# Second layer of a four-layer block: head norms' squares on ScalarE, forget gates among the keys' products, transposes between weight units, memory values a tile a step, output projections in two halves of the contraction

## The chip, the cores and the metric

One core of a Trainium2 chip runs the whole program once. The metric is device microseconds of that one execution, lower is better. TensorE (PE) multiplies and transposes, VectorE (DVE) and ScalarE (ACT) work on rows and read PSUM, GpSimd (POOL) works on SBUF only, and SyncE (SP) issues the weight loads.

## The reference, cut to what matters

Four layers over 256 tokens of width 1024, in fp32. Layers 0 and 1 have a mixer, a memory attention, an output projection and a squared-ReLU MLP. Layers 2 and 3 have two other mixers, an output projection and a gated MLP. The change concerns the mixer of layer 1 and the output projection of all four.

```python
# layer 1 (fox_group): forgetting attention with QK norm
proj = h @ w_in
q, k, v, f_logit, xq = jnp.split(proj, [512, 1024, 1536, 1544], axis=-1)
q = rms_norm(q.reshape(B, S, 8, 64), q_gain)
k = rms_norm(k.reshape(B, S, 8, 64), k_gain)
c = jnp.cumsum(jax.nn.log_sigmoid(f_logit + b_f), axis=1)      # causal, per head
s = q @ k.T / 8 + c[query] - c[key];  o = softmax(s) @ v
# memory_group: 4 heads of 128 into 256 memory tokens
k, v = jnp.split(rms_norm(mem, g_mem) @ w_kv, [512], axis=-1)
q = rms_norm(xq...);  k = rms_norm(k...);  y = softmax(q @ k.T / sqrt(128)) @ v
# every layer
x = x + jnp.concatenate([y_mix, y_mem], axis=-1) @ w_out
```

## The kernel before

**Products.** 256 tokens are two tiles `tt` of 128. An fp32 product is made of three fp32r products: high by high, high by low, low by high. Weights arrive in units of 128x1024 (two contraction tiles `j` of 512 columns). `unit` waits for a unit whose high part `whi` was made by ScalarE (`splits` there) and whose low part `wlo` by VectorE (`splits` there). There are NSPLIT = 4 buffers of each, and a buffer is released when the unit after it is begun (`unit_used`). A unit gives 12 products of 512 columns (2 `j`, 2 `tt`, 3 parts); a block of 512 output columns is four units, 48 products. `linear` and `block_of` go unit by unit over both tiles, `by_token` goes through all units for tile 0 and then for tile 1.

**Order.** Every engine runs a program written out by hand, in order. A wait at the head of an engine holds all that stands behind it. Both `splits` run ahead of PE by positions that the code sets: `full(name)` first makes the splits up to `AHEAD` = 3 units beyond the block it is about to read, and then waits for that block. The other waits on VectorE (`dve.wait_ge`) make no splits first.

**Layer 1, on PE:** block q by tile; both transposes of the normalised memory (`turn_norm(4, tt)`, banks 6 and 7, read out into MX); the forget gates f (24 contraction steps of 8 columns, 48 products); block k; the memory keys mk1; the cumulative sum c; blocks v and xq1; 32 transposes of the heads' rows (fqT, fkT) in four pieces; then `attend`. **The head norms** run on GpSimd: it squares 1024 columns into `hrow` (`headnorm`), VectorE sums them (`hsums`), GpSimd takes the power and scales the rows.

**Attention.** `attend` has ten steps here, six for the forgetting heads (fa) and four for the memory (ma1). Step n on PE: what `between` holds, scores of n+1, transposes of the probabilities of n, values of n-1. ScalarE (`soft`) makes the exponentials and copies the transposes, VectorE the maxima. The memory values mv1 are four whole units in `between` of steps 1 to 4.

**Output projection** (`out_proj`, `out_half`): columns 0 to 511 first, with all eight contraction tiles. Contraction tiles 4 to 7 come from the attention's rows, transposed last (`mo0`, `mo1`, `nr2`, `nr3`) and read out by ScalarE (MX_hi) and then VectorE (MX_lo). Columns 512 to 1023 follow by tile. Then comes the norm before the MLP.

Of the kernel before, what the change touches and what calls it, by code (L numbers as in the profile page):

```python
# [24 lines left out]
P = 128  # L25
# [61 lines left out]
def program(nc, a):  # L87
    ctx = ExitStack()
    with ctx:
# [127 lines left out]
        def memT(i, which):  # L217

            return slot(((9, 11), (7, 3))[i][which], 1024)
# [20 lines left out]
        def _(pe):  # L240
# [138 lines left out]

            def windows_by_unit(kv, flat):  # L380
# [62 lines left out]
            def out_rows(tag, tt, lo):  # L443

                turn(f"{tag}.{tt}", 6 + tt, [xn[:, tt, lo + j * P:lo + (j + 1) * P] for j in range(4)])
# [88 lines left out]
            def mem_ready(i):  # L534
                for tt in range(TT):
                    read_out(f"xqT{i}.{tt}")
                    read_out(f"mkT{i}.{tt}")
                    read_out(f"mv{i}.{tt}")
# [6 lines left out]
            def out_proj(L, w, k, first_half, late, second_half):  # L545


                names = [f"out{L}.0.0", f"out{L}.0.1"]
                first_half()
                linear(names, [0, 1], [a[w][0]], 2, tok(MX), 0, KT)  # L550
                late(0)
                linear(names, [0, 1], [a[w][1]], 2, tok(MX), 2, KT, opened=False)
                late(1)
                for tt in range(TT):
                    read_out(f"{second_half}.{tt}")
                linear(names, [0, 1], [a[w][2], a[w][3]], 2, tok(MX), 4, KT, opened=False)
                block_by_token(f"out{L}.1", w, 1, tok(MX), [2, 3], {(1, 3): lambda: turn_norm(k, 0)})

            def out_half(L, w, half, behind=None):


                linear([f"out{L}.0.{tt}" for tt in range(TT)], (0, 1), [a[w][2 * half + u] for u in range(2)], 2, tok(MX),
                       4 * half, KT, opened=(half == 0), behind=behind)
# [89 lines left out]
            for tt in range(TT):  # L653
# [8 lines left out]
            out_proj(0, "w_o0", 2, lambda: pe.wait_ge(ev("ylo"), 1),  # L662
                     lambda tt: (read_out(f"ma0.o{tt}"), out_rows("mo0", tt, 512)), "mo0")
# [19 lines left out]
            block_of("xq1", "w_b", 3, tok(XT), [0, 1])  # L683
            for n, s, e in (("fq", 4, "qaug"), ("fk", 7, "kaug")):
                pe.wait_ge(ev(e), 1)
                read_out("c")
                rows = slot(s, 1040).rearrange("p (t h d) -> p t h d", t=2, h=8)
                for tt in range(TT):
                    for half in range(2):
                        turn(f"{n}T.{tt}.{half}", 6 + half, [rows[:, tt, 4 * half + h, :] for h in range(4)])  # L690
# [8 lines left out]
            def mem_values(u):  # L699

                linear(["mv1.0", "mv1.1"], [2, 3], [a["w_kv1"][4 + u]], 2, tok(MX), 2 * u, KT, opened=(u == 0))
# [5 lines left out]
                "ma1": mem_spec(1)}, {**{1 + u: (lambda u=u: mem_values(u)) for u in (0, 2, 3)},  # L707
                                      2: lambda: (mem_values(1), mem_queries(1)), 5: lambda: (mem_keys(1), mem_ready(1)),
                                      9: lambda: [(read_out(f"fa.o{tt}"), out_rows("fo", tt, 0)) for tt in range(TT)]})
            out_proj(1, "w_o1", 5, lambda: [read_out(f"fo.{tt}") for tt in range(TT)],  # L710
                     lambda tt: (read_out(f"ma1.o{tt}"), out_rows("mo1", tt, 512)), "mo1")
# [3 lines left out]
            for L in (2, 3):  # L715
# [182 lines left out]
                def last_rows():  # L898
                    pe.wait_ge(ev("nrow"), i + 1)
                    out_rows(f"nr{L}", 1, 512)  # L900

                hgrn_read()
                out_half(L, f"w_o{L}", 0, {0: lambda: (read_out(f"co{L}.0"), out_rows(f"nr{L}", 0, 512)), 1: last_rows})
                for tt in range(TT):
                    read_out(f"nr{L}.{tt}")
                out_half(L, f"w_o{L}", 1)
                block_by_token(f"out{L}.1", f"w_o{L}", 1, tok(MX), [2, 3], {(1, 3): lambda: turn_norm(k + 1, 0)})
# [22 lines left out]
        def _(act):  # L930
# [233 lines left out]
            for tt in range(TT):  # L1164
                copy_out(f"q.{tt}", slot(0, 1024)[:, tt * BLK:(tt + 1) * BLK])
# [5 lines left out]
            for n, s in (("k", 1), ("mk1", 5), ("v", 2), ("xq1", 3)):  # L1171
                for tt in range(TT):
                    copy_out(f"{n}.{tt}", slot(s, 1024)[:, tt * BLK:(tt + 1) * BLK])
            for n, s in (("fq", 8), ("fk", 10)):
                dst = scr[:, s * SLOT:s * SLOT + 2048].rearrange("p (h t) -> p h t", h=8)
                for tt in range(TT):
                    for half in range(2):
                        copy_out(f"{n}T.{tt}.{half}", dst[0:65, 4 * half:4 * half + 4, tt * P:(tt + 1) * P],
                                 lambda ps: ps[0:65, :].rearrange("p (h t) -> p h t", h=4))
# [310 lines left out]
        def _(dve):  # L1490
# [316 lines left out]
            for tt in range(TT):  # L1807
                norm_rows(4, tt, slot(8 + tt, 1024))
# [444 lines left out]
```

## Time and profile before

| | us |
|---|---|
| median of 3 runs | 1411.62 |
| lowest, highest | 1409.45, 1412.41 |
| the profiled execution | 1406.15 |
| its span, first to last instruction | 1404.4 |
| PE busy in it | 1340.6 |
| DVE, ACT, POOL busy | 874.6, 712.6, 151.1 |

The profiled execution is one run and lies 5.5 us below the median of the three timed ones; 1.75 us of it lie outside the span. PE busy time counts a matmul from start to modelled end, so PE is hardly ever idle in the views and yet its pace depends on its granted clock.

### The profile page before, as it was taken

The numbers are of one execution on the slowest core, as the hardware profiler recorded it, in microseconds if no ns is written. First come the engines' busy times: TensorE is split into PE (matmuls) and PEld (weight loads), VectorE is DVE, ScalarE is ACT, GpSimd is POOL, SyncE is SP. The second block draws the span as 40 slices with busy tenths as digits, with TensorE's granted clock in tenths as the row PEclk, the third lists the DMA queues.
The fourth block names the chain that finished last, engine by engine and source line by source line (L and its number), as shares of the span: only waits on it lengthen the run. The fifth ranks groups of instructions, "written<-read, shape, count | busy, mean of one in ns | idle before, by whom it ended". The sixth has DMA issues, their size and how long they took to land.

```text
span 1404.4 us, 18621 instructions
## 1 busy us (share of the span) xinstructions
PE 1340.6 (95%) x7251; PEld 1136.1 (81%) x7251; DVE 874.6 (62%) x1146; ACT 712.6 (51%) x1167; POOL 151.1 (11%) x176
## 2 busy tenths in 40 slices
PE   6879999999998999999999999999999999999998
PEld 5657888887876788887988878888889887788887
DVE  4885656656443665656776556666677656666665
ACT  6465544545454554445653445555565444555553
POOL 2211100003340400002011011000021010100000
PEclk9989999998999999999999999999999999999999
DMA  9433655554521556554741136555556321466651
GB/s 374 140 119 97 232 196 192 168 181 157 172 92 60 195 169 206 191 184 152 242 135 60 61 105 208 187 190 190 166 170 208 112 61 60 140 194 194 193 194 46
DMA packets 62328, 224.44 MB, mean 160 GB/s; under 512 B 7192, under 2 KB 7328, under 8 KB 62240
## 3 DMA queue, kind: packets, MB, share of 16 engines
q1 hardware_dynamic: 59616, 214.23, 45.6%
q0 software_dynamic: 1904, 6.82, 1.5%
q10 hardware_dynamic: 720, 2.19, 0.4%
q8 instruction: 58, 0.95, 0.3%
q14 instruction: 30, 0.25, 0.1%
HBM read 222.16 MB, written 1.05 MB: 159 GB/s over the span
## 4 chain that ended last, share of the span: by engine, by line
PE 80%; DVE 11%; ACT 4%; issue 2%; POOL 2%; DMA 0%; POOLq 0%; DVEq 0%; ACTq 0%
PE ps L277 15%; PE ps L323 15%; PE ps L281 15%; PE ps L282 14%; PE ps L327 8%; PE ps L423 3%; DVE wlo L1502 2%; PE ps L330 2%; PE ps L481 2%; PE ps L458 2%; PE ps L753 2%; PE ps L329 1%; ACT scr L994 1%; DVE xn L1541 1%; POOL small L1327 1%
## 5 line engine op out<-in xcount | busy, mean ns | idle before, releaser
L1502 DVE TENSOR_TENSOR wlo<-raw,whi 128x1024 fp32r<-128x1024 f32 (+1 forms) x402 | 480.2, 1216 | 254.3 <-ACT whi L940 252.4
L940 ACT ACTIVATE whi<-raw 128x1024 fp32r<-128x1024 f32 (+1 forms) x409 | 424.3, 1048 | 314.6 <-PE ps L323 178.6
L323 PE MATMUL ps<-XT,whi 128*128 128x512 f32 x896 | 318.7, 399 | 0.0
L327 PE MATMUL ps<-XT,wlo 128*128 128x256 f32 x896 | 251.6, 281 | 0.0
L323 PEld LDWEIGHTS ps<-XT,whi 128*128 128x128 f32 x896 | 168.4, 188 | 41.1
L277 PE MATMUL ps<-whi,HT_hi 128*128 128x512 f32 (+1 forms) x496 | 187.8, 379 | 2.8 <-DVE wlo L1502 2.2
L282 PE MATMUL ps<-whi,HT_lo 128*128 128x512 f32 (+1 forms) x496 | 186.3, 376 | 0.0
L281 PE MATMUL ps<-wlo,HT_hi 128*128 128x512 f32 (+1 forms) x496 | 186.2, 375 | 0.0
L327 PEld LDWEIGHTS ps<-XT,wlo 128*128 128x128 f32 x896 | 169.2, 189 | 1.2
L277 PE MATMUL ps<-whi,XT 128*128 128x512 f32 (+2 forms) x352 | 141.2, 401 | 10.2 <-DVE wlo L1502 7.9
L281 PE MATMUL ps<-wlo,XT 128*128 128x512 f32 (+2 forms) x352 | 136.6, 388 | 0.0
L282 PE MATMUL ps<-whi,XT 128*128 128x512 f32 (+2 forms) x352 | 136.1, 387 | 0.0
L277 PEld LDWEIGHTS ps<-whi,HT_hi 128*128 128x128 f32 x496 | 93.2, 188 | 20.6 <-DVE wlo L1502 3.7
L282 PEld LDWEIGHTS ps<-whi,HT_lo 128*128 128x128 f32 x496 | 93.2, 188 | 17.4
L281 PEld LDWEIGHTS ps<-wlo,HT_hi 128*128 128x128 f32 x496 | 93.2, 188 | 16.9
L994 ACT ACTIVATE scr<-ps,small 128x256 f32<-128x256 f32 (+1 forms) x96 | 47.4, 502 | 98.8 <-DVE small L1591 87.3
L277 PEld LDWEIGHTS ps<-whi,XT 128*128 128x128 f32 x352 | 69.5, 198 | 28.4 <-DVE wlo L1502 11.1
L277 PE MATMUL ps<-whi,MX_hi 128*128 128x512 f32 x192 | 78.6, 410 | 14.0 <-issue 7.0
L1337 POOL TENSOR_SCALAR small<-small 128x1 f32<-128x1 f32 x20 | 11.0, 550 | 648.0 <-ACT xn L977 647.9
L282 PEld LDWEIGHTS ps<-whi,XT 128*128 128x128 f32 x352 | 69.4, 197 | 13.3
L281 PEld LDWEIGHTS ps<-wlo,XT 128*128 128x128 f32 x352 | 69.6, 198 | 10.3
L281 PE MATMUL ps<-wlo,MX_hi 128*128 128x512 f32 x192 | 76.1, 396 | 0.0
(252 smaller groups left out, 1871.3 us busy)
## 6 DMA issues: line engine op xcount, KB each, us to landing
raw<-in_w_m SPq DMA_DIRECT2D x152, 512.0 KB, 4.2
raw<-in_w_n SPq DMA_DIRECT2D x108, 512.0 KB, 4.2
raw<-in_w_c SPq DMA_DIRECT2D x48, 512.0 KB, 4.1
raw<-in_w_o SPq DMA_DIRECT2D x32, 512.0 KB, 3.6
raw<-in_w_kv SPq DMA_DIRECT2D x16, 512.0 KB, 4.6
raw<-in_w_b SPq DMA_DIRECT2D x16, 512.0 KB, 3.6
raw<-in_w_w SPq DMA_DIRECT2D x16, 512.0 KB, 5.0
raw<-in_w_a SPq DMA_DIRECT2D x12, 512.0 KB, 7.5
```

Source lines behind the costliest of these rows:

```text
L277: m = pe.matmul(out, xh, wh, start=first, stop=False)
L281: pe.matmul(out, xh, wl, start=False, stop=False)
L282: return pe.matmul(out, xl, wh, start=False, stop=last)
L323: m = pe.matmul(outs[f][:, :], hi[:, j, at], both, start=(k == 0), stop=False)
L327: pe.matmul(outs[f][:, 0:T], lo[:, j, at], XT[0][:, k, :], start=False, stop=False)
L330: m = pe.matmul(outs[f][:, :], hi[:, j, at], both, start=False, stop=True)
L423: m = pe.transpose(out[0:f, at:at + p], t, ident[0:p, 0:p])
L458: m = pe.matmul(out[:, j * klen:(j + 1) * klen], qT(h0 + j)[0:kd, tt * P:(tt + 1) * P], kT(h0 + j)[0:kd, 0:klen], start=(j == 0 or not cau ...
L481: m = pe.matmul(out[:, h * hd:(h + 1) * hd], turned(tag, n)[:, (j * kt + t) * P:(j * kt + t + 1) * P], V(h, t), start=(t == 0), stop=(t == ...
L940: act.activation(whi[:, g % NSPLIT, 0:w], raw[:, g % NRAW, 0:w], ACT.Copy).then_inc(split_hi, 1)
L994: m = act.activation(probs(tag, n)[:, j * klen:(j + 1) * klen], src, ACT.Exp, bias=sm(f"nmax{which}", 16)[:, c:c + 1], accum_out=sm(f"rsum ...
L1502: dve.tensor_tensor(wlo[:, g % NSPLIT, 0:w], raw[:, g % NRAW, 0:w], whi[:, g % NSPLIT, 0:w].bitcast(F32), ALU.subtract).then_inc(split_lo, 1)
```

## The change

Five edits in the programs of four engines.

1. **Head norms.** ScalarE squares each block out of PSUM, just before it copies it (`rows_in`). VectorE sums (`fox_sums`), GpSimd only takes the powers, and VectorE scales the rows (`scaled`). The gains become a per-partition column (`fgcol`, `mgcol`), made on VectorE after the logarithm and used as the scale of the copies of fkT and mkT.
2. **Gates among the keys** (`keys_and_gates`): the first keys' unit stands directly behind q; the 48 gate products stand in four groups of 12 among the second unit's; `turn_norm(4, 0)` and `turn_norm(4, 1)` follow the second and third unit.
3. **Turns between units**: the four pieces of fqT and fkT stand behind the four units of xq1.
4. **Memory values a tile a step**: eight pieces of six products (`by_tile`), the first behind the scores of step 0, the others woven into steps 0 to 5; the keys' transposes move from step 5 to 3, the forgetting rows' transposes from 9 to 8, and the first two units of the output projection go into steps 9 and 10.
5. **Output projections** of all layers: contraction tiles 0 to 3 for all 1024 columns (`out_first`, banks 0, 1 and 4, 5), then tiles 4 to 7 for all columns by tile (`out_second`).

```diff
+            def keys_and_gates():
+                names, tokens = ["k.0", "k.1"], tok(XT)
+                outs = [fill(n, b) for n, b in zip(names, (2, 3))]
...
+                for u in range(4):
+                    if u == 1:
+                        gf, fh, fl, _ = unit(a["w_f"][0], KT)
+                        forget = [fill(f"f.{tt}", 4 + tt) for tt in range(TT)]
+                    g, hi, lo, w = unit(a["w_b"][4 + u], 2)
...
+                    if u == 1:
+                        turn_norm(4, 0)
+                    if u == 2:
+                        turn_norm(4, 1)
-            def out_proj(L, w, k, first_half, late, second_half):
-                names = [f"out{L}.0.0", f"out{L}.0.1"]
-                first_half()
-                linear(names, [0, 1], [a[w][0]], 2, tok(MX), 0, KT)
-                late(0)
-                linear(names, [0, 1], [a[w][1]], 2, tok(MX), 2, KT, opened=False)
-                late(1)
-                for tt in range(TT):
-                    read_out(f"{second_half}.{tt}")
-                linear(names, [0, 1], [a[w][2], a[w][3]], 2, tok(MX), 4, KT, opened=False)
-                block_by_token(f"out{L}.1", w, 1, tok(MX), [2, 3], {(1, 3): lambda: turn_norm(k, 0)})
+            def out_first(L, w):
+                for nb, banks in enumerate(((0, 1), (4, 5))):
+                    names = [f"out{L}.{nb}.{tt}" for tt in range(TT)]
+                    for u in range(2):
+                        linear(names, banks, [a[w][4 * nb + u]], 2, tok(MX), 2 * u, KT, opened=(u == 0))
+                        yield
+            def out_second(L, w, k, rows):
+                for tt in range(TT):
+                    read_out(f"{rows}.{tt}")
+                late = lambda t, tt: tok(MX)(t + 4, tt)
+                by_token([([f"out{L}.{nb}.{tt}" for tt in range(TT)], None, [a[w][4 * nb + 2 + u] for u in range(2)], 2, late,
+                           False, True) for nb in range(2)], {(1, 3): lambda: turn_norm(k, 0)})
...
             block_by_token("q", "w_b", 0, tok(XT), [0, 1], after_norm(3), True)
-            for tt in range(TT):
-                turn_norm(4, tt)
-            linear(["f.0", "f.1"], [4, 5], [a["w_f"][0]], KT, tok(XT))
-            block_of("k", "w_b", 1, tok(XT), [2, 3])
+            keys_and_gates()
...
+            block_of("xq1", "w_b", 3, tok(XT), [0, 1],
+                     {0: lambda: heads_turned("fq", 4, 0), 1: lambda: heads_turned("fq", 4, 1),
+                      2: lambda: heads_turned("fk", 7, 0), 3: lambda: heads_turned("fk", 7, 1)})
...
+            def values_tile(n, s):
+                if (n, s) in ((0, 1), (1, 0), (2, 0), (3, 0), (4, 0), (5, 0), (5, 1)):
+                    next(values_left)
...
-                "ma1": mem_spec(1)}, {**{1 + u: (lambda u=u: mem_values(u)) for u in (0, 2, 3)},
-                                      2: lambda: (mem_values(1), mem_queries(1)), 5: lambda: (mem_keys(1), mem_ready(1)),
+                "ma1": mem_spec(1)}, {2: lambda: mem_queries(1), 3: lambda: mem_keys(1), 5: lambda: mem_ready(1, 2),
+                                      7: lambda: mem_ready(1), (8, 1): fox_rows, (9, 2): fox_out,
+                                      10: lambda: (mem_rows(0), next(out_left))},
+                   weave=values_tile, first=lambda: next(values_left))
...
+            def rows_in(name, sq, dst):
+                for tt in range(TT):
+                    at = slice(tt * BLK, (tt + 1) * BLK)
+                    ps = full(f"{name}.{tt}")
+                    act.activation(sq[:, at], ps[:, :], ACT.Square).then_inc(ev("sqf"), 1)
+                    copy_out(f"{name}.{tt}", dst[:, at])
...
+            def fox_sums(n, dst, sq, hd):
+                dve.wait_ge(ev("sqf"), 2 * n)
+                dve.tensor_reduce(dst, sq.rearrange("p (n d) -> p n d", d=hd), AX.X, ALU.add).then_inc(ev("fsum"), 1)
+            def scaled(dst, src, r, n, hd, event):
+                dve.wait_ge(ev("frstd"), n)
+                dve.tensor_tensor(dst, src.rearrange("p (n d) -> p n d", d=hd), bc(r, 2, hd), ALU.mult).then_inc(ev(event), 1)
+            squares_ = hrow[:, :, :].rearrange("p a b -> p (a b)")
+            fox_sums(1, sm("rq16", 16), squares_, 64)
             for tt in range(TT):
                 norm_lo(4, tt, MX)
+            qa = slot(4, 1040).rearrange("p (n d) -> p n d", d=65)
+            dve.memset(qa[:, :, 64:65], 1.0)
+            scaled(qa[:, :, 0:64], slot(0, 1024), sm("rq16", 16), 1, 64, "qaug")
...
+            splits(fills["k.1"].pos + AHEAD)
+            fox_sums(2, sm("rk16", 16), slot(10, 1024), 64)
```

**VectorE where block q ends and the keys begin.** The rows are VectorE's instructions in program order. The four `xn<-scr` normalise the memory rows, `wlo` 128x64 is the gates' unit, and each `wlo` 128x1024 is the low part of a weight unit that PE needs. Before, they read:

```order
L1541 SCALAR_TENSOR_TENSOR xn<-scr,small,gain 128x512 x4
L1502 TENSOR_TENSOR wlo<-raw,whi 128x64
L1502 TENSOR_TENSOR wlo<-raw,whi 128x1024 x2
L1525 TENSOR_TENSOR MX_lo<-ps,MX_hi 128x4x128 x4
L1502 TENSOR_TENSOR wlo<-raw,whi 128x1024
```

After:

```order
L1615 SCALAR_TENSOR_TENSOR xn<-scr,small,gain 128x512 x4
L1887 TENSOR_REDUCE small<-hrow 128x16
L1576 TENSOR_TENSOR wlo<-raw,whi 128x1024
L1576 TENSOR_TENSOR wlo<-raw,whi 128x64
L1576 TENSOR_TENSOR wlo<-raw,whi 128x1024 x4
L1599 TENSOR_TENSOR MX_lo<-ps,MX_hi 128x4x128 x2
L1576 TENSOR_TENSOR wlo<-raw,whi 128x1024
L1599 TENSOR_TENSOR MX_lo<-ps,MX_hi 128x4x128 x2
```

The first keys' unit is now the first `wlo` 128x1024, and the sum over q's squares stands ahead of it; the seventh unit of this list (counting the gates') is the memory keys' second.

**VectorE behind the logarithm of the gates.** The last rows of the logarithm are those of 128x16; what follows is the low part of the memory keys' third unit. Before:

```order
L1696 TENSOR_SCALAR small<-small 128x16
L1823 TENSOR_SCALAR small<-small 128x16
L1824 TENSOR_TENSOR small<-small 128x16
L1502 TENSOR_TENSOR wlo<-raw,whi 128x1024 x8
L1827 TENSOR_SCALAR scr<-ps 128x16
```

After:

```order
L1914 TENSOR_TENSOR small<-small 128x16
L1917 TENSOR_TENSOR small<-rowg 128x64
L1918 TENSOR_TENSOR small<-small,const 128x64
L1919 TENSOR_REDUCE small<-small 128x1
L1920 MEMSET small 1x1
L1921 TENSOR_TENSOR small<-rowg 128x128
L1922 TENSOR_TENSOR small<-small,const 128x128
L1923 TENSOR_REDUCE small<-small 128x1
L1576 TENSOR_TENSOR wlo<-raw,whi 128x1024
L1887 TENSOR_REDUCE small<-scr 128x16
L1576 TENSOR_TENSOR wlo<-raw,whi 128x1024 x4
```

Seven instructions for the two gain columns and the keys' sum have moved in among the low parts; before, the logarithm stood ahead of the low part of the keys' fourth unit and of the seven after it.

**PE at the first attention step, after.** `scr` rows are scores (128x128) and transposes, the 128x512 by `HT_hi` is the mask, `whi` and `wlo` are the first tile of the memory values.

```order
L490 MATMUL ps<-scr 128x128 x4
L494 MATMUL ps<-HT_hi 128x512
L277 MATMUL ps<-whi,MX_hi 128x512
L281 MATMUL ps<-wlo,MX_hi 128x512
L282 MATMUL ps<-whi,MX_lo 128x512
L277 MATMUL ps<-whi,MX_hi 128x512
L281 MATMUL ps<-wlo,MX_hi 128x512
L282 MATMUL ps<-whi,MX_lo 128x512
L490 MATMUL ps<-scr 128x128 x4
```

Before, the two groups of scores stood next to each other, and the first memory value unit followed the first transposes. On VectorE the maximum of step 0 stands ahead of this unit's `wlo` in both kernels.

## Rows read from the trace of the kernel before

**Rows 1.** The page: TensorE's granted clock in 40 slices of the span, tenths.

```profile
PEclk9989999998999999999999999999999999999999
```

**Rows 2.** Waits of PE, 325 to 470 us: total, times, longest.

```profile
PE ps L423 <- DVE MX_lo L1525: 3.4, 2, 1.7
PE ps L423 <- ACT scr L955: 3.2, 5, 1.2
PE ps L458 <- ACT scr L955: 2.3, 2, 1.2
PE ps L277 <- issue: 1.5, 1, 1.5
PE ps L277 <- DVE wlo L1502: 1.3, 2, 0.9
PE ps L423 <- ACT scr L994: 1.2, 1, 1.2
```

**Rows 3.** Busy time per engine in stretches; third from last the clock.

```profile
340.00:345.00 5.00, 5.00 (x22) 4.81 (x23) 0.79 (x5) 0.35 (x2) 0.00 (x0) 0.50 0.33 111
345.00:350.00 5.00, 5.00 (x14) 3.84 (x13) 3.74 (x16) 0.97 (x2) 0.00 (x0) 0.50 0.00 0
430.00:435.00 5.00, 4.99 (x35) 4.25 (x34) 2.50 (x6) 3.65 (x13) 0.00 (x0) 1.00 0.02 3
```

**Rows 4.** Timeline of PE, q's end to v's begin: start, duration, operation.

```profile
332.58 0.40 PE L282 MATMUL ps<-whi,XT 128*128 128x512 f32 x1
...
336.53 0.25 PE L277 MATMUL ps<-whi,XT 128*128 128x8 f32 x1
...
339.66 0.28 PE L281 MATMUL ps<-wlo,XT 128*128 128x8 f32 x1
...
357.73 0.39 PE L277 MATMUL ps<-whi,MX_hi 128*128 128x512 f32 x1
...
369.19 0.48 PE L277 MATMUL ps<-whi,XT 128*128 128x512 f32 x1
```

**Rows 5.** Timeline of PE: eight transposes between products.

```profile
317.23 1.04 PE L423 MATMUL ps<-const,xn 128*128 128x128 f32 x8
318.02 0.48 PE L277 MATMUL ps<-whi,HT_hi 128*128 128x512 f32 x1
```

**Rows 6.** Timeline of DVE: memory rows' low part, logarithm's ends, a sum.

```profile
336.91 1.29 DVE L1525 TENSOR_TENSOR MX_lo<-ps,MX_hi 128x512 fp32r<-128x512 f32 x2 [0.91 <-ACT MX_hi L961]
...
344.02 0.17 DVE L1816 TENSOR_TENSOR small<-ps,rowg 128x8 f32<-128x8 f32 x1 [0.47 <-PE ps L282]
...
347.92 0.18 DVE L1824 TENSOR_TENSOR small<-small 128x16 f32<-128x16 f32 x1
...
376.09 1.22 DVE L1572 TENSOR_REDUCE small<-hrow 128x16 f32<-128x1024 f32 x1 [5.41 <-POOL hrow L1358]
```

**Rows 7.** Timeline of ACT: the copy of q's second tile.

```profile
333.01 0.60 ACT L955 ACTIVATE scr<-ps 128x512 f32<-128x512 f32 x1
```

**Rows 8.** Timeline of PE: heads' transposes, scores of steps 0 and 1.

```profile
392.24 1.04 PE L423 MATMUL ps<-const,scr 128*65 128x128 f32 x8
393.56 1.14 PE L423 MATMUL ps<-const,scr 128*65 128x128 f32 x8 [0.29 <-ACT scr L955]
...
398.63 1.13 PE L458 MATMUL ps<-scr 65*128 65x128 f32 x8 [1.20 <-ACT scr L955]
```

**Rows 9.** Timeline of DVE: maximum of step 0 and splits behind it.

```profile
400.03 0.69 DVE L1587 TENSOR_REDUCE small<-ps 128x4 f32<-128x512 f32 x1 [15.67 <-PE ps L462]
400.63 3.49 DVE L1502 TENSOR_TENSOR wlo<-raw,whi 128x1024 fp32r<-128x1024 f32 x3
```

**Rows 10.** Waits of PE in the whole span, for the output projections.

```profile
PE ps L277 <- issue: 7.0, 5, 1.5
```

**Rows 11.** Timeline of PE in layer 0: a long wait for a low part.

```profile
79.58 0.47 PE L277 MATMUL ps<-whi,MX_hi 128*128 128x512 f32 x1 [2.96 <-DVE wlo L1502]
...
80.34 0.62 PE L277 MATMUL ps<-whi,MX_hi 128*128 128x512 f32 x1
```

More of the change, by code:

```diff
@@ L217, in memT @@
         def memT(i, which):
-            return slot(((9, 11), (7, 3))[i][which], 1024)
+            return slot(((9, 11), (7, 4))[i][which], 1024)
         xflat = xn[:, :, :].rearrange("p t d -> p (t d)")
@@ L543, in mem_spec, with out_proj @@
                         lambda h, t: mv[:, t * BLK + h * P:t * BLK + (h + 1) * P], [2, 3])
[L545 to L563 removed]
+            def out_first(L, w):
[5 more added lines that the diff above has]
+            def out_second(L, w, k, rows):
+                for tt in range(TT):
+                    read_out(f"{rows}.{tt}")
+                late = lambda t, tt: tok(MX)(t + 4, tt)
+                by_token([([f"out{L}.{nb}.{tt}" for tt in range(TT)], None, [a[w][4 * nb + 2 + u] for u in range(2)], 2, late,
+                           False, True) for nb in range(2)], {(1, 3): lambda: turn_norm(k, 0)})
+            def out_proj(L, w, k, late, rows):
+                left = out_first(L, w)
+                for tt in range(TT):
+                    next(left)
+                    late(tt)
+                for _ in left:
+                    pass
+                out_second(L, w, k, rows)
             def mlp(L, w_in, w_out, blocks, kts, squared, k, first=(4, 5)):
@@ L1177, in _, with mem_keys_in @@
                     for half in range(2):
-                        copy_out(f"{n}T.{tt}.{half}", dst[0:65, 4 * half:4 * half + 4, tt * P:(tt + 1) * P],
-                                 lambda ps: ps[0:65, :].rearrange("p (h t) -> p h t", h=4))
+                        ps = full(f"{n}T.{tt}.{half}")
+                        kw = {"scale": sm("fgcol", 1)[0:65, :]} if n == "fk" else {}
+                        free(f"{n}T.{tt}.{half}", act.activation(
+                            dst[0:65, 4 * half:4 * half + 4, tt * P:(tt + 1) * P],
+                            ps[0:65, :].rearrange("p (h t) -> p h t", h=4), ACT.Copy, **kw))
+            rows_in("xq1", squares_, slot(3, 1024))
+            def mem_keys_in():
+                for tt in range(TT):
+                    ps = full(f"mkT1.{tt}")
+                    free(f"mkT1.{tt}", act.activation(
+                        memT(1, 1).rearrange("p (h t) -> p h t", h=4)[:, :, tt * P:(tt + 1) * P],
+                        ps[:, :].rearrange("p (h t) -> p h t", h=4), ACT.Copy, scale=sm("mgcol", 1)))
             def mem_rows_in():
```

147 lines of the change are left out of this document (87 added, 60 removed).

## The prediction

> **What bounds the kernel now.** I read the page first. PE is busy in 1340.6 of the span of 1404.4 us (the table), and its clock is granted in full but for a few slices [rows 1]. Its work is not changed: every product of before is there after, in another order. So a gain can come only from PE's waits and from its stretches at half clock, and a loss only from new ones. The second view is the waits of PE in layer 1 [rows 2]: 12.9 us. The third is the clock in stretches of 5 us: 0.50 in 340 to 350 [rows 3], which is the lower of its two levels (1.2 GHz for 2.4). What PE did before: a wait of 1.7 us for MX_lo [rows 2] and then products of 8 columns [rows 4]. At half clock 10 us of work are 5 of it; about 4.9 us are lost there. The waits of the output projections are the "issue" rows [rows 10]: four of them are 1.53 us, one in each layer; PE stands there until the last transposed rows are read out by ScalarE and VectorE.
>
> All sums below are made against the profiled execution (1406.15 us, span 1404.4) and then put on the median of the runs, 1411.62, which lies 5.5 us higher.
>
> **1. From q to the memory keys.** Before, PE begins q's last product at 332.58 and the memory keys at 357.73 [rows 4]; q's end at 332.81 makes 24.9 us. After, the work is: 48 products of 512 columns, 48 of 8 columns, two groups of eight transposes. From mk1's begin at 357.73 to v's at 369.19 are 48 wide products and the small ones of c [rows 4], so 48 take some 10.9 us (0.227 each). From 336.53 to 339.66 are 28 narrow ones [rows 4], 0.112 each, 5.4 us for 48. Eight transposes in the midst of products take 0.79 us and make the next product 0.1 longer [rows 5]: 1.8 for two groups. Together 18.1 us at full clock, with neither the wait of 1.7 nor the half clock.
>
> But there is a new wait in front. The keys' first unit now stands directly behind q, and VectorE makes its low part only after the sum of q's squares, as the order in the section on the change shows, and the sum waits for the square of q's second tile. Before, this unit was not wanted until the gates were done. q's last product ends at 332.98 (332.58 + 0.40) [rows 4], ScalarE is there at 333.01 and a pass over 128x512 of PSUM takes 0.60 [rows 7]: square done at 333.6. The sum takes 1.22 [rows 6], the low part 1.22 (a little over a third of the 3.49 for three) [rows 9], the second begins 0.1 before the first ends: 336.0. PE begins at 336.07, 3.1 us after q's last end. So mk1 begins at 336.07 + 18.1 = 354.2 instead of 357.73: **3.5 us gained**. Bounds: a wait of 2.0 us (the square and sum overlapping more than I see) gives 4.6; for the clock see rival A.
>
> **2. The memory keys and what stands behind.** With X the begin of the keys' fourth unit (right behind the last transposes), PE wants mk1's third unit at X + 2.75 + 2 x 2.75 = X + 8.25. VectorE: the memory rows' low part ended 1.67 us after the transposes before (336.91 + 1.29 against 336.53) [rows 4, 6], so X + 1.67; clearing a column 0.1; scaling q, a pass over 128x1024 like a low part, 1.2: X + 2.95. Then bias and logarithm: from the second bias to the end 344.02 to 348.10, 4.1 us [rows 6], and 0.15 for the first bias: X + 7.2. Seven operations on 64 and 128 columns for the gains: each 0.18 like the ones of 16 columns [rows 6] and up to 0.12 more for the columns, with the 0.03 between them 1.8: X + 9.0. Low part 1.2: X + 10.2. **PE waits 1.9 us** in mk1, where it waited for nothing. Bounds 1.2 (small operations at 0.18) and 2.6 (twice the seven's excess). Gone is the wait of 0.87 in v, since VectorE stood then for GpSimd's squares (5.41 us) [rows 6] and these are gone. Net **1.0 us lost**. The keys' sum and the scaling of k and mk1, 1.2 us each, find 2.75 us per unit of which a low part takes 1.2; four buffers hide them. ScalarE's eight squares, 0.6 each, come beside its copies; a unit costs it one split in 2.75 us and it is busy in half the span (the table); hidden. The cover would be gone only if they stood in front of a split that PE wants next, which is so for none but the one above.
>
> **3. Turns of the heads.** From 392.24 to 398.63, 6.4 us [rows 8]. After: four times 0.9 [rows 5] and the wait of 1.20 for the last copies, which stays [rows 8], and 0.25 of drain: 5.0. **1.4 us gained**. The copies of fk carry a scale column; bound 0.2 us on the last wait.
>
> **4. Attention.** Of the 12.9 us of rows 2, 1.7 are part 1's, 1.3 for `wlo` are v's 0.9 and 0.4 before the MLP, which stays; the heads have 1.20 and three short ones like the 0.29 [rows 8], 0.8 together. 7.9 us are left, six waits of 1.1 to 1.7: for the exponentials of step 0, the memory keys' copies (two), around the forgetting rows' transposes (two), and before the output projection's second half. All lie where no unit's products stand; now tiles or units do, or (the last) 5.5 us of units. New ones: (a) the first memory tile stands behind the scores of step 0, and its low part on VectorE behind the maximum of step 0. That maximum begins at 400.03 and what follows it at 400.63 [rows 9]; 1.22 later is 401.85, while PE is through with the scores and the mask when the maximum begins: **1.9 us**, since low part and maximum must both be waited for. (b) the second piece of xqT needs bank 7, whose copy stands behind a split and two exponentials on ScalarE: about 0.7, bounds 0 and 1.5. (c) the transposes of step 9 stand behind ScalarE's two MX_hi and exponentials, 0.4. Net 7.9 - 3.0 = **4.9 us gained**.
>
> **5. Output projections of layers 0, 2 and 3.** 1.53 us each [rows 10], now behind two units (5.5 us): **4.6 us gained**. The norm behind them has the same way as before, since the last four pieces by tile take as long as those of the second half did; its additions of the first columns come later, 2.7 us before the second ones, enough for the 0.7.
>
> **Sum:** 3.5 - 1.0 + 1.4 + 4.9 + 4.6 = 13.4 us. I keep 1 us back for short waits that come with 20 new switches between operations. 1411.62 - 12.4 = **1399.2 us** (as a profiled run 1393.8).
>
> **The clock.** In the profile a wait of 2.96 us was followed by half clock (the same product 0.47 long at 79.58 and 0.62 at 80.34) [rows 11], while attention steps without filler, full of small operations, held the full one at 430 to 435 [rows 3]. So the gates among wide products should hold it, and the new wait of 3.1 us need not. The Trainium skill, "TensorE: Matmul & The Clock Gate", section "Why this matters for your kernels", warns of idle gaps of PE between bursts, after which its clock falls; the trace has the case above for it. By that rule rival A is the forecast; I leave it second, since a wait may fall so that it is diluted by the dense products on both sides, which it has here.
>
> **Rivals.** *A. The clock falls at the new wait.* For: [rows 11]. Once for 3 to 4 us it costs 1.7; if it holds on through the gates (the narrow products held it down before) [rows 3] 8.1 us of unit two become 16.2, so up to 9. The time is 1401 to 1408. Chance 0.22. *B. The new waits of 3.1, 1.9 and 1.9 do not show,* since VectorE is earlier than I work out; then 6.9 us more: 1392. Against it stands the order of VectorE, which is fixed. Chance 0.07. *C. No change:* the units moved up meet late low parts wherever a wait vanished, as in (a), each for its like; 1411.6. It needs 12 us more in waits of 1 to 2, some seven more places than I find. Chance 0.04. *D. Slower: the clock at half from the new wait to the end of mk1.* Transposes and gates keep it down and the wait in mk1 comes before it has risen. Work of 18.1 + 10.9 us at full clock doubles: 29 us, 15.7 more than the gain, 1428; it decides from 26 us at half clock on. Against: after the gates 14 wide products at half clock brought it back before [rows 3]. Chance 0.03; 0.02 more for other losses. The forecast itself, with its own range of 1394.5 to 1403, has 0.62.
>
> **The numbers.** 0.2% (2.8 us) is about what a measurement of this kernel can tell from no change. Bounds of the forecast: 1.1 in part 1, 0.7 in 2, 1.0 in 3 and 4 each way, and 2 us since the timed runs lie up to 2.2 us off their median. The range 1393.5 to 1406 takes the forecast and most of A, leaving out 0.17. Faster 0.92 (forecast, A, B), same 0.03, slower 0.05.
>
> **What would show it.** Right: PE's first wide product with XT after q waits some 3 us for `wlo` of VectorE, with a sum from `hrow` right before it there; a wait of 1.9 in mk1 behind seven small operations; one of 1.9 behind the mask of step 0; no "issue" wait of 1.5 in any layer; the clock 1.00 during the gates. Wrong: half clock there (A), or several waits for `wlo` in the output projections, which would mean that their units come sooner than the splits can.

## The result, and the profile after

The changed kernel takes 1406.12 us in the median of 20 runs (1390.98 to 1407.63), the kernel before 1409.88 in 20 runs beside them (1404.70 to 1412.41). The ratio is 0.9969, 95% interval 0.9955 to 0.9983: 4.4 us faster by it (3.8 by the two medians), where 12.4 were forecast. The profiled execution took 1405.79, its span is 1403.7, with a mean granted clock of 0.979; before, 1404.4 and 0.985.

The page after, PE's line and the clock in 40 slices, against [rows 1]:

```profile
PE 1345.6 (96%) x7251; PEld 1141.0 (81%) x7251; DVE 877.5 (63%) x1156; ACT 716.4 (51%) x1175; POOL 131.3 (9%) x163
...
PEclk9999999997999999999999999999999998999999
```

The waits of PE from 325 to 470 us in the changed kernel, against [rows 2]:

```profile
PE ps L277 <- DVE wlo L1576: 7.2, 4, 3.2
PE ps L490 <- ACT scr L1254: 1.4, 1, 1.4
PE ps L455 <- ACT scr L1058: 0.5, 1, 0.5
PE ps L455 <- ACT scr L1019: 0.3, 1, 0.3
```

They are 9.4 us instead of 12.9; 0.5 of the difference is a wait of block q for `wlo` that lies just inside this window before (325.87) and just outside it after (323.47). The timeline of PE after: the last unit of layer 0's output projection, then q's end and the gates, then three later waits (against [rows 4, 8]):

```profile
127.09 0.50 PE L277 MATMUL ps<-whi,MX_hi 128*128 128x512 f32 x1 [0.56 <-DVE wlo L1576]
...
330.18 0.39 PE L282 MATMUL ps<-whi,XT 128*128 128x512 f32 x1
333.73 0.76 PE L277 MATMUL ps<-whi,XT 128*128 128x512 f32 x1 [3.17 <-DVE wlo L1576]
...
338.56 0.63 PE L282 MATMUL ps<-whi,XT 128*128 128x512 f32 x1
...
339.80 0.25 PE L277 MATMUL ps<-whi,XT 128*128 128x8 f32 x1
...
340.79 0.40 PE L281 MATMUL ps<-wlo,XT 128*128 128x512 f32 x1
...
343.21 0.63 PE L282 MATMUL ps<-whi,XT 128*128 128x512 f32 x1
...
345.20 0.35 PE L282 MATMUL ps<-whi,XT 128*128 128x8 f32 x1
...
366.56 0.50 PE L277 MATMUL ps<-whi,MX_hi 128*128 128x512 f32 x1 [1.49 <-DVE wlo L1576]
...
399.84 1.13 PE L490 MATMUL ps<-scr 65*128 65x128 f32 x8 [1.43 <-ACT scr L1254]
...
403.37 0.77 PE L277 MATMUL ps<-whi,MX_hi 128*128 128x512 f32 x1 [2.01 <-DVE wlo L1576]
```

The waits stand where they were forecast and have nearly the sizes forecast: 3.17 behind q (3.1), 1.49 in mk1 (1.9), 2.01 in step 0 (1.9). But the same wide product takes 0.63 us behind the wait at 338.56, 0.40 at 340.79, and 0.63 again at 343.21 in the midst of the gates, and a narrow one goes from 0.25 to 0.35. Those are the two levels of the clock. The same stretch in windows, with the clock third from last (against [rows 3]):

```profile
330.00:335.00 5.00, 1.83 (x6) 1.25 (x5) 3.62 (x4) 2.08 (x4) 2.99 (x3) 0.76 0.40 133
335.00:340.00 5.00, 5.00 (x18) 4.04 (x18) 1.22 (x1) 1.35 (x2) 2.65 (x1) 0.55 0.95 338
340.00:345.00 5.00, 5.00 (x32) 4.63 (x31) 1.23 (x1) 0.35 (x1) 0.00 (x0) 0.79 0.43 161
345.00:350.00 5.00, 5.00 (x22) 4.71 (x22) 0.00 (x0) 0.00 (x0) 0.00 (x0) 0.50 0.00 0
350.00:355.00 5.00, 5.00 (x21) 4.25 (x21) 2.77 (x4) 3.20 (x4) 0.00 (x0) 0.69 0.17 46
...
400.00:405.00 5.00, 2.99 (x13) 2.27 (x13) 3.60 (x4) 3.48 (x12) 0.00 (x0) 0.59 0.11 25
```

Between q and the memory keys 17.1 us are at half clock, where 10.2 were before and none was forecast: 6.8 from 332.6, which is inside PE's wait (330.57 to 333.73), and 10.2 from 342.9, among the gates (338.99 to 350.03). Another 6.8 us from 400.9 lie about the two waits at the attention's begin.

Why the waits are there is read from DVE's timeline after, against [rows 6, 9]: the addition to x stands ahead of the projection's last low part, the sum of q's squares ahead of the keys' first, the gains' operations ahead of mk1's third, the maximum of step 0 ahead of the first memory value unit's.

```profile
125.21 0.69 DVE L1627 TENSOR_TENSOR x<-ps,x 128x512 f32<-128x512 f32 x1 [2.84 <-PE ps L282]
125.82 1.22 DVE L1576 TENSOR_TENSOR wlo<-raw,whi 128x1024 fp32r<-128x1024 f32 x1
...
331.23 1.22 DVE L1887 TENSOR_REDUCE small<-hrow 128x16 f32<-128x1024 f32 x1 [1.24 <-ACT hrow L1234]
332.37 2.48 DVE L1576 TENSOR_TENSOR wlo<-raw,whi 128x1024 fp32r<-128x1024 f32 x3
...
363.57 0.22 DVE L1917 TENSOR_TENSOR small<-rowg 128x64 f32<-128x64 f32 x1
...
365.29 1.22 DVE L1576 TENSOR_TENSOR wlo<-raw,whi 128x1024 fp32r<-128x1024 f32 x1
...
401.40 0.69 DVE L1661 TENSOR_REDUCE small<-ps 128x4 f32<-128x512 f32 x1 [14.66 <-PE ps L494]
402.00 3.49 DVE L1576 TENSOR_TENSOR wlo<-raw,whi 128x1024 fp32r<-128x1024 f32 x3
```

In the output projections the four "issue" waits of 1.53 us [rows 10] are gone, and a new one of 0.56 stands in each.

The two profiles by stage. The stages end at the begin of q's last product, of mk1, of the attention's first scores, of the products behind layer 2's first wait of 1.52 us (734.43 before, 732.65 after), and at the end of the span:

| stage ends at | before, us | after, us | difference | forecast | at half clock, before / after |
|---|---|---|---|---|---|
| q's last product | 332.58 | 330.18 | -2.4 | -1.5 | 10.2 / 6.8 |
| mk1 | 25.15 | 29.29 | **+4.1** | -3.5 | 10.2 / 17.1 |
| attention | 40.90 | 40.37 | -0.5 | -0.4 | 0 / 0 |
| layer 2's wait | 335.80 | 332.81 | -3.0 | -4.9 | 0 / 6.8 |
| end | 669.97 | 671.05 | **+1.1** | -3.1 | 20.5 / 27.3 |

At half clock are 41.0 us before and 58.0 after, which costs 8.5 us more than before. The forecast of the profile was -13.4 before the reserve: 4.9 of it was half clock regained, and 8.5 was waits. The profile shows -0.7. With the 8.5 lost to the clock put aside that is -9.2, close to the 8.5 forecast for the waits. So what lies between forecast and profile, 12.7 us, is the clock: 8.5 lost in place of 4.9 regained.

The sum can be put to the runs, too, since each has its own span and mean clock. A run loses about (1 - clock) x span to half clock; the rest is the span at full clock. In the median that rest is 1382 us for the kernel before (the 17 runs beside the first experiments) and 1374.3 after (20 runs): 7.6 gained. The loss to the clock is 25.4 before and 29.5 after. So 7.6 - 4.1 = 3.5 us are left, about what was measured. Each clock is given to 0.001, so the two parts of a single run are known to about 0.7 us.

### The profile page after: what moved, and what is told of

It is laid out like the page before. It is cut to its first block, busy times and chain, and to the rows that moved or that the text cites. A ratio compares the mean times of both kernels' runs of the same rounds, so it can differ in the third digit from the quotient of the medians.

```text
span 1403.7 us, 18627 instructions
## 1 busy us (share of the span) xinstructions
PE 1345.6 (96%) x7251; PEld 1141.0 (81%) x7251; DVE 877.5 (63%) x1156; ACT 716.4 (51%) x1175; POOL 131.3 (9%) x163
## 4 chain that ended last, share of the span: by engine, by line
PE 79%; DVE 12%; ACT 4%; issue 2%; POOL 2%; DMA 0%; POOLq 0%; DVEq 0%; ACTq 0%
PE ps L323 15%; PE ps L277 15%; PE ps L282 14%; PE ps L281 14%; PE ps L327 8%; DVE wlo L1576 3%; PE ps L455 3%; PE ps L330 2%; PE ps L513 2%; PE ps L490 2%; PE ps L818 2%; PE ps L329 1%; ACT scr L1058 1%; DVE xn L1615 1%; DVE x L1627 1%
## 5 line engine op out<-in xcount | busy, mean ns | idle before, releaser
L277 PE MATMUL ps<-whi,MX_hi 128*128 128x512 f32 x192 | 80.4, 419 | 12.4 <-DVE wlo L1576 10.4
L282 PEld LDWEIGHTS ps<-whi,XT 128*128 128x128 f32 x352 | 69.6, 198 | 13.4
L281 PEld LDWEIGHTS ps<-wlo,XT 128*128 128x128 f32 x352 | 69.8, 198 | 10.2
L282 PE MATMUL ps<-whi,MX_lo 128*128 128x512 f32 x192 | 77.4, 403 | 0.0
```

Of the source, the lines that this page charges most:

```text
L277: m = pe.matmul(out, xh, wh, start=first, stop=False)
L281: pe.matmul(out, xh, wl, start=False, stop=False)
L282: return pe.matmul(out, xl, wh, start=False, stop=last)
```

## The experiments

**Theory 1:** TensorE's clock falls at its idle time behind q, and products there would hold it. **Theory 2:** the gates' narrow products bring it down by themselves. All kernels but projection_halves_alone, which is made from the kernel before, are made from the changed kernel. The kernel before ran beside them: 1411.02 us in the median of 17 runs for the experiments 1 to 4, 1410.81 (14 runs) for 5 to 8, 1409.90 (18 runs) for the next three and 1411.02 (9 runs) for the last. The last two columns are on the mean granted clock of each kernel's runs.

| kernel | median us | ratio, 95% | median clock | runs at 0.987 or above |
|---|---|---|---|---|
| the changed kernel | 1406.12 | 0.9969 (0.9955-0.9983) | 0.979 | 2 of 20 |
| projection_halves_alone | 1407.56 | 0.9986 (0.9972-1.0) | 0.981 | 0 of 11 |
| q_sum_behind_splits | 1395.69 | 0.9898 (0.9877-0.992) | 0.9865 | 2 of 4 |
| gates_over_two_units | 1402.08 | 0.9936 (0.9917-0.9955) | 0.984 | 0 of 6 |
| splits_and_two_units | 1398.92 | 0.9922 (0.9904-0.994) | 0.985 | 0 of 4 |
| wait_filled | 1398.08 | 0.9895 (0.9857-0.9932) | 0.9855 | 3 of 6 |
| gates_as_before | 1405.12 | 0.9954 (0.9938-0.9969) | 0.979 | 0 of 9 |
| early_value_half | 1391.69 | 0.9858 (0.9834-0.9882) | 0.988 | 3 of 6 |
| four_orders_mended | 1387.72 | 0.9829 (0.9802-0.9857) | 0.9865 | 3 of 6 |
| four_waits_filled_b | 1398.37 | 0.993 (0.9906-0.9955) | 0.989 | 5 of 7 |
| late_waits_filled_b | 1408.27 | 0.9989 (0.9963-1.0014) | 0.980 | 1 of 12 |
| mended_and_filled_b | 1386.80 | 0.9834 (0.9821-0.9846) | 0.991 | 3 of 4 |
| mended_one_fill | 1386.01 | 0.9824 (0.9804-0.9844) | 0.986 | 1 of 5 |

**1. The sum of q's squares behind the low parts.** On VectorE:

```diff
             squares_ = hrow[:, :, :].rearrange("p a b -> p (a b)")
+            splits(fills["q.1"].pos + AHEAD)
             fox_sums(1, sm("rq16", 16), squares_, 64)
```

> The changed kernel, with VectorE making the low parts of the keys' first unit, the gates' unit and the keys' second ahead of the sum of q's squares. Everything else stays. The wait of 3.17 us behind q should go in every theory. Theory 1 (the wait alone brings the clock down, the gates among wide products can hold it): half clock goes from the whole stretch 332 to 353, about 3.2 + 3.4 + 5.1 = 11.7 us less than the changed kernel, ratio to the kernel before about 0.989. Theory 2 (twelve narrow products between three wide ones bring it down by themselves): only the wait and the first fall go, 6.6 us less, ratio about 0.992, and half clock still stands in the gates.

1395.69 us, 10.4 less than the changed kernel for one line. By its time alone it is nearer to theory 1 (11.7 less) than to theory 2 (6.6 less). The wait behind q is 0.70 instead of 3.17. The windows of this run:

```profile
330.00:335.00 5.00, 4.30 (x20) 3.27 (x19) 4.48 (x6) 3.68 (x6) 1.10 (x2) 1.00 0.16 64
335.00:340.00 5.00, 5.00 (x36) 4.57 (x35) 2.83 (x3) 1.06 (x1) 4.04 (x2) 1.00 0.95 369
340.00:345.00 5.00, 5.00 (x29) 4.68 (x27) 0.00 (x0) 0.00 (x0) 0.00 (x0) 0.64 0.49 200
345.00:350.00 5.00, 5.00 (x21) 4.29 (x22) 2.61 (x3) 3.18 (x4) 0.00 (x0) 0.68 0.09 25
```

The clock holds at 1.00 where the wait was, and still falls at 341.4, in the gates, for 6.8 us. So both theories have a part. Of the 17.1 us 10.3 are gone here, but how they divide between wait and gates is not firm: with the same order from q to the gates the stretch in the gates is 3.4 to 13.7 us in the five profiles that have it (experiments 1, 7, 8, 11 and 12). Nor is all of the 10.4 us won in this stage. In the profiles this stage takes 22.6 us for 29.3, 6.7 less, and the span is 9.4 shorter: 2.0 are lost ahead of q's end and 4.6 won behind the first scores. The program is the same in both places, but the clock is not: behind the first scores 22.1 us are at half clock instead of 34.1.

**2 and 3. The gates over two units,** eight groups of six products in the keys' second and third unit instead of four of twelve in the second, with the wait (2) and without it (3):

```diff
-                            if u == 1:
-                                for kf in range(4 * j, 4 * j + 4):
+                            if u in (1, 2):
+                                at = 4 * (u - 1) + 2 * j
+                                for kf in range(at, at + 2):
...
```

> The changed kernel, with the 48 gate products in eight groups of six among the keys' second and third unit in place of four groups of twelve in the second. The wait behind q stays. Theory 1: the clock falls at the wait as before and the gates matter little, so less than 2 us gained. Theory 2 (the density of narrow products counts): the first fall at the wait stays, the second over the gates goes, about 5 us less than the changed kernel, ratio to the kernel before about 0.993.

> Both edits: low parts ahead of q's sum, and the gates over two units. Theory 1: like the first alone, 11.7 us less than the changed kernel. Theory 2: 11.7 us less too, and clearly more than the first alone (by 5). Ratio to the kernel before about 0.989 in both; what tells them apart is the first edit alone.

With the wait, one stretch at half clock is left there, 6.8 us from 334.4, inside the wait of 3.17 (it ends at 335.58). With the wait down to 0.69 none is left; the windows of run 3:

```profile
340.00:345.00 5.00, 5.00 (x38) 4.59 (x36) 1.29 (x2) 1.09 (x2) 0.00 (x0) 1.00 0.16 64
345.00:350.00 5.00, 4.96 (x28) 3.93 (x27) 2.95 (x4) 2.98 (x4) 0.00 (x0) 1.00 0.14 34
```

That is each theory at its own place in the profile: one stretch goes with the wait, the other with the dense gates. The other profiles agree:

| between q and the memory keys | profiles | the clock falls |
|---|---|---|
| PE idle for 3.2 to 4.2 us behind q | 4 | inside the wait in 4 |
| 0.7 us idle there, or filled | 8 | ahead of the gates in 0 |
| gates in groups of twelve among wide products | 9 | in the gates in 8, 0.1 us behind them in 1 |
| gates in groups of six | 2 | in the gates in 0 |
| all 48 gate products in a row, behind 1.7 us idle (the kernel before, and 4) | 2 | in the gates in 2 |

The groups of six rest on two profiles only. In the time, 2 is 4.0 below the changed kernel, as theory 2 has it (5), where theory 1 had less than 2. 3 is 7.2 below it, where both theories had 11.7, and 3.2 above 1 (the intervals overlap). Run 3 reaches the first scores 3.1 us earlier than run 1 (392.00 against 395.06) in spite of a new wait for MX_lo of 0.97 and one for `wlo` of 2.09 instead of 1.50, and gives it back later. From layer 2's wait to the end it takes 670.5 us and run 1 667.0, with the same program there: 28.6 us at half clock against 18.7.

**4. The kernel before with the projections' contraction in halves alone** (`out_first`, `out_second` and the new `out_proj` in place of the old one, in all four layers; the attention and the order up to it as before).

> The kernel before with only the output projections in two halves of the contraction, in all four layers. Prediction's term: 1.53 us in each layer, 6.1 us in all, ratio 0.9957. By the trace of the changed kernel a wait of 0.56 us for the last low part has come in its place in each layer: 4 times 0.97, 3.9 us, ratio 0.9972. If the clock elsewhere is not touched, no more and no less.

1407.56, a ratio of 0.9986 that touches 1. The rest at full clock is 1377.8 in the median against 1381.9 for the kernel before beside it: 4.1 us gained, about four times 1.53 - 0.56. Half of it does not show in the time, since the clock's loss is 26.7 instead of 25.4 in the median and, in the profiled run, 29.0 instead of 20.5. That run has 6.8 us at half clock from 400.9 like the changed kernel, although nothing of layer 1's attention was changed; its waits there are 1.20 and 0.77. So the changed kernel's two waits are not shown to be the cause of its stretch there.

**5. The wait behind q filled.** The changed kernel with 14 products that nobody reads, written into the bank that the keys open next:

```diff
             outs = [fill(n, b) for n, b in zip(names, (2, 3))]
+            for _ in range(14):
+                pe.matmul(outs[0][:, :], XT[0][:, 0, 0:P], XT2[:, 0, :, :].rearrange("p s t -> p (s t)"), start=True, stop=True)
```

> The changed kernel with 14 products of 128x512 that nobody reads, put into the idle 3.17 us between q and the keys; waits and order stay as they are. If it is TensorE's idle time behind q that brings its clock down (theory 1), the 6.8 us at half clock from 332.8 go, worth 3.4 us, and some of the 10.2 us behind them may go too: 1403 or less, a ratio of 0.994 to 0.990, with the 3.17 us wait shown as busy. If the narrow products of the gates bring it down by themselves (theory 2), or the fillers delay the keys as much as they give, the time stays at 1406, 0.997.

1398.08, 8.0 below the changed kernel, although no wait for data is shorter and PE has 14 products more to do. Three of the six runs have a clock of 0.991 or 0.992 and take 1390 to 1393 us, the other three 0.979 or 0.980 and 1403 to 1405. The profile is of one of the latter. PE's timeline (the first row are the 14):

```profile
329.24 3.33 PE L386 MATMUL ps<-XT 128*128 128x512 f32 x14
332.48 0.50 PE L277 MATMUL ps<-whi,XT 128*128 128x512 f32 x1
...
335.47 0.25 PE L282 MATMUL ps<-whi,XT 128*128 128x8 f32 x1
...
338.71 0.35 PE L282 MATMUL ps<-whi,XT 128*128 128x8 f32 x1
...
339.50 0.63 PE L281 MATMUL ps<-wlo,XT 128*128 128x512 f32 x1
```

The wide products behind the filled wait are at full clock, and the clock falls among the gates, for 13.7 us from 338.3. In windows:

```profile
330.00:335.00 5.00, 5.00 (x23) 3.91 (x22) 4.46 (x5) 1.59 (x3) 3.53 (x2) 1.00 0.59 194
335.00:340.00 5.00, 5.00 (x33) 4.58 (x32) 1.62 (x2) 1.06 (x1) 1.50 (x1) 0.83 0.99 362
340.00:345.00 5.00, 5.00 (x22) 4.61 (x20) 0.00 (x0) 0.00 (x0) 0.00 (x0) 0.50 0.18 73
```

So the filling removes the wait's own stretch, as theory 1 has it, and the gates' is theory 2's. The stage itself takes 28.2 us for 29.3 in this profile, with 13.7 at half clock for 17.1; most of the 8.0 comes from the three runs at 0.991 or 0.992, of which there is no profile.

**6. The gates as before,** ahead of the keys' first unit, all else as changed:

```diff
-            keys_and_gates()
+            for tt in range(TT):
+                turn_norm(4, tt)
+            linear(["f.0", "f.1"], [4, 5], [a["w_f"][0]], KT, tok(XT))
+            block_of("k", "w_b", 1, tok(XT), [2, 3])
```

> The changed kernel with the gates' products back ahead of the keys' first unit, and both turns of the memory's norm ahead of them; all else as changed. If moving the gates in among the keys' products gains something (theory A: the gates' narrow products find company), this is 2 to 4 us slower than the changed kernel: 1408 to 1410, 0.998 to 1.000. If the half clock stands there either way, since the wait behind q is ahead of both orders (theory B), it is within 1 us of it: 1406, 0.997.

1405.12, as theory B has it; the interval (0.9938 to 0.9969) overlaps that of the changed kernel (0.9955 to 0.9983). The wait behind q is 4.17, now for MX_lo (329.08 to 333.24), and 17.1 us are at half clock from 331.5 on. Putting the gates among a single unit's products was worth nothing that these runs can tell.

**7. The first memory value unit's low part ahead of step 0's maximum,** on top of 1:

```diff
-                    ps = full(f"{tag}.s{i}", 0)
+                    ps = full(f"{tag}.s{i}", 1 if n == 0 and tags[0] == "fa" else 0)
```

> The run with the sum of q's squares behind the low parts, and also the low part of the first unit of memory values ahead of step 0's maximum. Theory: the 2.00 us wait in step 0 goes, and with it the 3.4 us at half clock from 399.6, worth 1.7: 1392 against 1395.7, a ratio of 0.9875. Rival: the maximum and with it step 0's probabilities come 1.2 us later and TensorE waits for them instead, so 1395 to 1396, 0.990.

1391.69, 4.0 below run 1 and at the first expectation. PE goes from the mask into the values at 396.38 without a wait:

```profile
395.92 0.66 PE L494 MATMUL ps<-HT_hi 128*128 128x512 f32 x1
396.38 0.63 PE L277 MATMUL ps<-whi,MX_hi 128*128 128x512 f32 x1
```

The maximum stands at 396.62, 0.70 behind the mask's start against 0.67 (400.73 to 401.40) in the changed kernel: the low part was done before, and the maximum is no later. The rival is out. The 3.4 us at half clock stayed, now from 396.0, so that part of the expectation failed, and the time agrees with it partly by luck: 2.0 us are the wait, and the other 2 us are within the spread of the runs.

**8. Four orders mended:** besides 1 and 7, the seven gain operations behind `scaled(ka...)`, and in the output projections:

```diff
-                residual(rows, 0, 1)
+                residual(rows, 0, 2 if rows[0:3] == "out" else 1)
...
```

> The run before this one, and also the gains' column operations moved from ahead of the keys' sums to behind the scaling of the keys, and in every output projection the low part of the last unit ahead of the addition to x. Theory: the wait in the memory keys (1.50) and the four waits of 0.56 go, 3.7 us in all: 1388.5, a ratio of 0.985. Rival 1: the turned keys of fox need the gains' column and wait for it, 1390 to 1392. Rival 2: the stretches at half clock in layers 2 and 3 fall otherwise and take or give some 3 us.

1387.72, as expected; neither the wait in mk1 nor any of 0.56 is left. All waits for low parts in the whole span:

```profile
PE ps L277 <- DVE wlo L1576: 14.7, 16, 2.6
```

That is 14.7 us against 22.7 (22 waits) in the changed kernel. In the median over the runs, 7.3 of the 18.4 us below the changed kernel are at full clock (1367.0 for 1374.3) and 10.8 are a smaller loss to the clock (18.7 for 29.5). The profiled run has 13.7 us at half clock in the gates where run 7 has 6.8, with the same order there.

**9 to 12. Further fillings.** `busy(bank, n)` writes n such products into a bank that is free and opened next.

```diff
+                        busy(7, 8)
                         pe.wait_ge(ev("nrow"), i + 1)
```

> The changed kernel with products of 128x512 that nobody reads in its waits: 14 behind q, 6 ahead of the attention's first scores (1.43 us), 9 ahead of the first unit of memory values (2.01 us), and 8 ahead of the last turned rows in layers 2 and 3 (1.77 us each). All waits for data stay. Theory 1 (idle TensorE brings its clock down): the mean granted clock of most runs is 0.988 or more, the 6.8 us at half clock from 401 and some of the 27 us in layers 2 and 3 go, and the median is 1390 to 1395, 0.988. Rival 1: only the wait behind q counts, 1398 as in that run alone. Rival 2: products in a wait do nothing lasting, and the run with 14 of them was lucky: 1405 to 1406.

> The changed kernel with 8 unread products ahead of the last turned rows in layers 2 and 3 alone, nothing filled behind q. Theory 1: of the 6.8 us at half clock from 807.3 and from 1182.7 at least half goes, 3.4 us in all: 1402.5, 0.994, and layer 1 stays as it is. Rival: the stretches there come from the narrow turns and the small products round them: 1406, 0.997.

> The kernel with all four orders mended, and the unread products ahead of the attention's first scores and of the last turned rows in layers 2 and 3. Theory 1: the clock is 0.99 in most runs instead of some: 1382 to 1384, 0.980. Rival: as without them, 1387.7, 0.983, or slower by the products that outlast their wait.

> The kernel with all four orders mended, and 6 unread products ahead of the attention's first scores (1.43 us) alone, without those of layers 2 and 3, which fell outside the wait that they were meant for and cost 8 x 0.21 = 1.7 us each. Theory: the mended and filled kernel's 1386.8 less 3.4, 1383.4, ratio 0.981. Rival: the products in layers 2 and 3 held the clock up after all, and without them the time goes back to 1387.7 or above, 0.983 or more.

The products of layers 2 and 3 missed their wait: it is for the first tile's rows, and they stand behind the first unit. In the run with these alone:

```profile
807.18 0.80 PE L461 MATMUL ps<-const,xn 128*128 128x128 f32 x4 [1.77 <-DVE xn L2184]
...
818.61 1.98 PE L252 MATMUL ps<-XT 128*128 128x512 f32 x8
```

So late_waits_filled_b (expected 1402.5, or 1406 by its rival) says nothing on that wait. It became a control: more unread products, not in a wait, give no better clock (0.980; 1 of 12 runs) and cost their time, 1408.27; its rest at full clock is 1377.7, 3.4 above the changed kernel's. four_waits_filled_b has the clock that theory 1 expected, 0.989 in four of seven runs, but not the time: 1398.37 is what the first rival had. It carries the same 3.4 us of useless work, and without them would be at some 1395 by this estimate. Its profile is its slowest run (1410.19, clock 0.979); the stretches in layers 2 and 3 stand in it, and there is none of a run at 0.989. mended_and_filled_b came out at 1386.80 instead of 1382 to 1384, nearer to its rival's 1387.7. mended_one_fill came out at 1386.01 instead of 1383.4, 1.7 below four_orders_mended, within the spread of both. The three mended versions cannot be told apart; each beats both kernels by 18 to 25 us.

## Why the prediction was wrong

It was on the right side, but 3.8 us were gained (by the two medians) of 12.4 forecast, and the time of 1406.1 lies a little above its range. The time flatters it by 1.7 us: it was put on 1411.62, the median of three runs of the kernel before, which is 1409.88 in 20. By its own steps:

- **Part 1, the order on VectorE: right.** The wait is 3.17 for 3.1, with the sum of `hrow` right ahead.
- **Part 1, the clock: this step failed.** It said that the gates among wide products should hold the clock and the wait of 3.1 us "need not" bring it down, and booked 4.9 us as regained. The stage took 29.3 us for 21.6 forecast; 17.1 of them are at half clock, worth 8.5. Its reason was that the dense products on both sides dilute the wait; they stood on both sides, and the clock fell inside the wait, at 332.6. Rival A named the first cause, and its price of "up to 9" and times of 1401 to 1408 are what was measured; it should have been the forecast. The row from which I argued against it [rows 3], 430 to 435 us, has attention products in it, and the waits nearest to it are of 1.1 to 1.2 us: it was not the like of this place, while the wait of 2.96 with half clock behind it [rows 11] was. The rule of the Trainium skill that the prediction cites ("TensorE: Matmul & The Clock Gate", section "Why this matters for your kernels") is that the clock falls after idle gaps of PE between bursts of products. The traces agree: all four profiles with a wait of 3.2 us or more behind q fall to half clock inside it, and none of the eight without it falls ahead of the gates.
- But A alone is not enough. Run 3 is the only one without half clock between q and the keys, and it needs both: no wait, and gates in groups of six. In runs 1 and 5, without a long idle wait, the clock fell within the groups of twelve. The prediction had the narrow products, in its rivals, only as what holds a clock down that has already fallen.
- **Part 2: a size off.** 1.49 for 1.9; stage as forecast (-0.5 for -0.4).
- **Part 3: near.** Parts 2 and 3 share a stage of -0.5; the waits of part 2 are +0.6 of it (1.49 come, 0.87 gone), which leaves 1.1 gained for 1.4. The wait for the last copies is 1.43 for 1.20.
- **Part 4: the waits right, the clock not.** New waits 2.01 (1.9), 0.3 (0.7), 0.5 (0.4). The stage gained 3.0 of 4.9; the 6.8 us at half clock from 400.9 stand at two waits of 3.4 us in sum (their cause is not shown, see 4).
- **Part 5: mis-sized by a third.** 1.53 became 0.56, so 0.97 was gained each time, not 1.53; run 8 took the rest away.
- **The point that was not in the sum:** time lost to the clock in layers 2 and 3, whose programs differ in nothing but the projection, 20.5 us at half clock before and 27.3 after in the two profiles, and 18.7 and 28.6 in runs 1 and 3. They vary between kernels that have the same program there, so the difference is not shown to be the edit's.

What stays open: why the same kernel has runs at 0.979 and at 0.991, 12 to 15 us apart, and why filling 3 us in layer 1 changes the share of the latter, which is more than the stretch behind q itself can give (3.4 us). Counted over kernels the tie is plain, its mechanism is not: where PE's idle wait behind q is under 1 us or filled, 20 of 42 runs have a clock of 0.987 or above; in the other changed kernels it is 3 of 47, in projection_halves_alone 0 of 11, in the kernel before 1 of 58. The cause of the stretches in layers 2 and 3 stays open too: the unread products meant for them missed their wait.

## What to carry to other kernels

Price a new wait of TensorE by what the clock costs behind it as well as by its own length: here one line that put the low parts ahead of a sum took a wait from 3.2 to 0.7 us and the median down by 10.4; in the profiles 6.7 of that is won in the stage, and the rest where the clock stood better later on. When work moves so that a unit is wanted earlier, walk the engine that prepares it for what stands ahead (a sum, a maximum, an addition, seven small operations): all four such places were mended for 18 us in all, of which 8 were waits for low parts and the rest the clock. A profile pair whose mean clocks differ by 0.006 differs by 8 us in 1404 for that alone; put each run's (1 - clock) x span aside before judging an edit by its time.

## What was not expected of the hardware

- The clock falls among dense narrow products with PE never idle: in wait_filled the profile has PE busy 5.00 of 5.00 us in every window from 330 to 355, and products of 128x8 go from 0.25 to 0.35 us. With groups of six between wide ones (splits_and_two_units) it stayed at 1.00.
- The same program on the same chip ran at 0.979 to 0.992 in different runs (wait_filled: 1390.40 to 1404.94 us), and the kernel before between 0.977 and 0.987.
- Useless products in an idle wait made a kernel 8 us faster in the median of six runs, by a better clock in three of them.
